# PEER expert lookup: tiles 2 to 8 gather first row halves only; second halves are read densely, times a coefficient matrix

## The reference, cut to what matters

```python
s = jnp.einsum('thpd,phkd->pthk', qh, p['pk_sub_keys'])      # scores against 2 x 128 keys
sv, si = lax.top_k(s, PK_TOPK)
cand = sv[0][..., :, None] + sv[1][..., None, :]             # 256 sums per head
best, pos = lax.top_k(cand, PK_TOPK)
eidx = ...                                                   # si[0] * 128 + si[1] of the best
gate = jax.nn.softmax(best, axis=-1)
act = jax.nn.gelu(jnp.einsum('td,thkd->thk', hb, u_tab[eb]))
out = jnp.einsum('thk,thkd->td', gb * act, v_tab[eb])
```

## Time and profile before

| | us |
|---|---|
| median of 3 runs (3966.49 to 3968.9) | 3967.75 |
| span of the profiled execution | 3962.1 |
| first dot product | 881.7 |
| DVE reads the sums of tile 1 (group 128) | 1608.3 |
| the same of tile 3 (group 256), tile 4 (group 320), tile 8 (group 576) | 2308.1, 2643.6, 3949.6 |
| PE, DVE, POOL, ACT busy | 2943.4, 2784.1, 1319.1, 676.6 |
| moved by the gathers' queue | 1208 MB |

### The profile page before, as it was taken

One profiled execution on the slowest core, in us unless ns is written; L12 is line 12 of the kernel. 1 busy time (PEld: TensorE's weight loads), 2 busy tenths in 40 slices (PEclk: granted clock), 3 DMA queues, 4 the chain that ended last, 5 costly groups with the idle time before them and its releaser, 6 DMA issues.

```text
span 3962.1 us, 46323 instructions
## 1 busy us (share of the span) xinstructions
PE 2943.4 (74%) x16906; PEld 1316.2 (33%) x16906; DVE 2784.1 (70%) x6805; ACT 676.6 (17%) x1388; POOL 1319.1 (33%) x1174
## 2 busy tenths in 40 slices
PE   8999999979899997856666666656656666665555
PEld 3666665545444442213222222212212222221111
DVE  4545647746787786756888868877877786887555
ACT  2534533011121221000111110111101111101000
POOL 0000000014444443333444444444544444444443
PEclk9999999989899998988878878878877878886777
DMA  4010004459999999999999999999999999999998
GB/s 184 23 35 26 23 25 157 170 207 410 413 415 414 408 403 415 418 423 413 414 396 413 418 416 409 416 410 420 415 411 414 418 414 408 415 416 407 418 421 343
DMA packets 214904, 1346.40 MB, mean 340 GB/s; under 512 B 24818, under 2 KB 45810, under 8 KB 63762
## 3 DMA queue, kind: packets, MB, share of 16 engines
q0 software_dynamic: 165888, 1208.03, 74.2%
q1 hardware_dynamic: 47636, 133.32, 9.0%
q10 hardware_dynamic: 1152, 2.10, 0.1%
HBM read 1329.69 MB, written 13.67 MB: 339 GB/s over the span
## 4 chain that ended last, share of the span: by engine, by line
DMA 37%; PE 35%; DVE 13%; issue 11%; POOL 2%; ACT 1%; POOLq 0%; SPq 0%; DVEq 0%; ACTq 0%
DMA arena<-in_uv,mask_b 14%; PE ps L782 12%; DMA arena<-in_uv,mask_f 12%; DMA arena<-in_uv,ones 11%; PE ps L1453 9%; DVE arena L1294 4%; PE ps L760 3%; PE ps L647 3%; POOL arena L616 2%; DVE arena L1176 2%; PE ps L1447 2%; PE ps L711 1%; PE ps L678 1%; DVE arena L1136 1%; PE ps L1505 1%
## 5 line engine op out<-in xcount | busy, mean ns | idle before, releaser
L782 PE MATMUL ps<-arena 64*64 64x512 f32 x9216 | 1461.6, 761 | 943.0 <-DVE arena L1176 929.3
L1294 DVE CUSTOM_DVE_ANT_0 arena<-arena 128x1024 f32<-128x1024 f32 x1152 | 1411.7, 1226 | 738.3 <-DMA arena<-in_uv,mask_b 285.1
L782 PEld LDWEIGHTS ps<-arena 64*64 64x64 f32 x9216 | 351.4, 158 | 1896.4 <-DVE arena L1176 1380.3
L616 POOL DMA_INDIRECT arena<-in_uv,ones x384 | 448.3, 1167 | 635.0 <-PE ps L782 467.4
L616 POOL DMA_INDIRECT arena<-in_uv,mask_f x384 | 441.8, 1150 | 586.7 <-PE ps L782 493.4
L616 POOL DMA_INDIRECT arena<-in_uv,mask_b x384 | 423.2, 1102 | 601.9 <-PE ps L782 514.6
L973 ACT ACTIVATE arena<-arena 128x2 f32<-128x2 f32 x576 | 117.3, 204 | 2641.0 <-DVE arena L1294 2565.6
L1453 PE MATMUL ps<-arena 128*128 128x384 f32 x1152 | 384.1, 489 | 1.8 <-DVE arena L1740 1.8
L1176 DVE TENSOR_SCALAR arena<-arena 128x64 f32<-128x64 f32 x1152 | 308.0, 310 | 0.3 <-ACT arena L973 0.3
L760 PE MATMUL ps<-arena 128*128 128x384 f32 x768 | 268.6, 497 | 0.0
L598 POOL IOTA arena<- 128x16 f32 x1 | 0.1, 145 | 793.3 <-PE ps L660 793.3
(11 more groups left out here) (203 smaller groups left out, 2360.7 us busy)
## 6 DMA issues: line engine op xcount, KB each, us to landing
arena<-in_w_mg SPq DMA_DIRECT2D x16, 1536.0 KB, 21.2
arena<-in_w_in SPq DMA_DIRECT2D x28, 512.0 KB, 3.3
arena<-in_w_mod SPq DMA_DIRECT2D x8, 1792.0 KB
arena<-in_w_mod SPq DMA_DIRECT2D x4, 2048.0 KB, 23.3
arena<-in_w_out SPq DMA_DIRECT2D x2, 4096.0 KB, 16.8
arena<-in_w_q SPq DMA_DIRECT2D x8, 1024.0 KB, 14.2
arena<-in_w_q SPq DMA_DIRECT2D x4, 2048.0 KB
arena<-x_scratch SPq DMA_DIRECT2D x15, 512.0 KB, 11.2
```

The costliest lines, as they stand in the source:

```text
L616: nc.gpsimd.indirect_dma_start(out=RG[n % RING], out_offset=None, in_=uv, in_offset=bass.IndirectOffsetOnAxis(ap=EIDX[t % 3][:, s:s + 1], ...
L782: mm = nc.tensor.matmul(PS[c * HALF:(c + 1) * HALF, 2 * r + n, :], DG[rows, s, :], RG[s][rows, D + n * 512:D + (n + 1) * 512], start=(g == ...
L1294: ins = v.tensor_tensor_reduce(u, u, h2, 1.0, 0.0, ALU.mult, ALU.add, PRE[:, s % RING:s % RING + 1])
```

## The change

Tiles 0 and 1 stay as they are. Tiles 2 to 8 are handled in four **teams**: (2, 3), (4, 5), (6, 7), (8).

- POOL gathers only the u halves, 4 KB a row, into six buffers `UB`. DVE's dot product frees a buffer. The dots of a tile are kept (`DOTS`); ACT takes one gelu per tile, DVE one product with the gates (`coefs`).
- When a team's dots are done, its **coefficient matrix** is built: `COEF[i2, i1, token]`, for 128 x 128 experts and up to 256 tokens. `turn` transposes key numbers and coefficients. For every four tokens (a **block**) DVE makes one-hots of both key numbers (`key_hots`, 512 columns each), ACT scales one of them (`scale_part`), PE multiplies them per token (`block`) and ACT stores the result (`block_out`). Two buffers each. There are 32 blocks a tile, two blocks a group, from `build_at(g)` = 258, 386, 514 and 638.
- Then `values`: SP loads v in 128 chunks of 128 rows (`chunk`, 0.5 MB, four buffers), PE multiplies each with the matrix. The ends of a team (`ends_at` = build_at + 112 groups) read PSUM on DVE. The matrix has one buffer, and the buffers of the ends lie in it: the next team's first block waits for the stored outputs.
- `mix`, `x1` and the norms of tiles 3 to 8 now stand at groups 117 to 156. The **late queries** of all six tiles are taken head pair by head pair (`late_query`: 384-column matmuls, weights in two buffers of 2 MB; `late_score` six per pair), every score goes through the scratch, and ACT loads it. The top-16 search of tiles 3 and 4 stands at groups 170 to 256, that of later tiles where it was. The ends of tiles 0 and 1 stand at groups 224 to 241.

```diff
+TEAMS = ((2, 3), (4, 5), (6, 7), (8,))
...
-MIX_AT, MIX_STEP = 117, 3
+MIX_AT, MIX_GAP = 117, 6
+LATE_QUERIES_AT, LATE_QUERIES_GAP = 158, 11
 EARLY_TOP_AT = {(0, 0): None, (0, 1): 0, (0, 2): 18, (0, 3): 27, (1, 0): 37, (1, 1): 47, (1, 2): 65, (1, 3): 78,
-                (2, 0): 90, (2, 1): 100, (2, 2): 110, (2, 3): 129}
-LATE_AT = {3: 2 * GROUPS + 24}
-LATE_GAP = {3: 10}
+                (2, 0): 90, (2, 1): 100, (2, 2): 110, (2, 3): 129,
+                (3, 0): 170, (3, 1): 181, (3, 2): 192, (3, 3): 203,
+                (4, 0): 214, (4, 1): 225, (4, 2): 236, (4, 3): 247}
+A_ENDS_AT = 224
...
+    VB = [hi(0), hi(1), AR[:, A_END - 2 * D:A_END - D], AR[:, A_END - D:A_END]]
+    UB = [AR[:, A_WO + n * D:A_WO + (n + 1) * D] for n in range(UR)]
+    assert A_WO + UR * D == A_END - 2 * D
+    FULL = [hi(2 + n)[:, 0:512].rearrange("p (u i) -> p u i", u=4) for n in range(2)]
+    PART = [hi(2 + n)[:, 512:1024].rearrange("p (u i) -> p u i", u=4) for n in range(2)]
...
+    def build_at(g):
+        done = (TEAMS[g][-1] + 1) * GROUPS + 2
+        return max(done, ends_at(g - 1) + 12) if g else done
...
+        return build_at(g) + 112
...
+        def query_weights(i):
+            sp.dma_start(WQB[i % 2], w_q[:, :, i * 512:(i + 1) * 512]).then_inc(l_wqb[i % 2], 16)
...
+        def chunk(g, i1):
+            n = g * P + i1
+            if n >= VR:
+                sp.wait_ge(v_done, n - VR + 1)
+            sp.dma_start(VB[n % VR], uv[i1 * P:(i1 + 1) * P, D:2 * D]).then_inc(l_v[n % VR], 16)
...
+                    if m < UR:
+                        wait_alone(pool, v_used, n + 1 - RING)
+                    else:
+                        wait_alone(pool, dots, (n - UR) // GRP + 1)
+                    nc.gpsimd.indirect_dma_start(
+                        out=UB[m % UR], out_offset=None, in_=u_rows,
+                        in_offset=bass.IndirectOffsetOnAxis(ap=EIDX[t % 3][:, s:s + 1], axis=0),
+                    ).then_inc(u_in[m % UR], 16)
...
+        def late_query(i, c, part):
+            n = (i * 4 + c) * 2 + part
+            if c == 0 and part == 0:
+                pe.wait_ge(l_wqb[i % 2], 16 + 16 * (i // 2 + 1))
+                if i == 0:
+                    pe.wait_ge(h2t_e, TILES)
+            if n >= 2:
+                pe.wait_ge(lq_e, n - 1)
+            cols = slice(part * LATE_PART, (part + 1) * LATE_PART)
             for k in range(KD):
-                mm = nc.tensor.matmul(PS[:, 4, c * P:(c + 1) * P], WQ[:, k, (i * 4 + c) * P:(i * 4 + c + 1) * P],
-                                      H2T[:, k, :], start=(k == 0), stop=(k == KD - 1))
-            if c == 3:
-                mm.then_inc(q_r, 1)
+                mm = nc.tensor.matmul(PS[:, 4 + part, 0:LATE_PART], WQB[i % 2][:, k, c * P:(c + 1) * P],
+                                      H2TB[:, k, cols], start=(k == 0), stop=(k == KD - 1))
+            mm.then_inc(lq_r, 1)
...
+        def turn(t):
+            g, j = team_of(t)
+            pe.wait_ge(coef_r, t - NA + 1)
+            if t == NA:
+                pe.wait_ge(sc_e, len(QUERY_ORDER) + PAIRS * (TILES - EARLY))
+                pe.wait_ge(lq_e, PAIRS * 8)
+            elif j == 0:
+                pe.wait_ge(tu_e, t - NA)
+            for z, x in enumerate((*KEYNO[(t - NA) % 4], DOTS[t % 2])):
+                mm = nc.tensor.transpose(PS[:, 4 + 2 * j, z * P:(z + 1) * P], x, ident[:])
+            mm.then_inc(tu_r, 1)
+        def block(g, n):
+            b_, k = n % 2, blocks_before[g] + n
+            pe.wait_ge(part_r, k + 1)
+            if k >= 2:
+                pe.wait_ge(c_r, k - 1)
+            for u in range(4):
+                mm = nc.tensor.matmul(PS[:, 5 + 2 * b_, u * P:(u + 1) * P], FULL[b_][:, u], PART[b_][:, u],
+                                      start=True, stop=True)
+            mm.then_inc(built, 1)
+        def values(g):
+            pe.wait_ge(c_r, blocks_before[g + 1])
+            if g:
+                pe.wait_ge(acc_read, TEAMS[g][0] - NA)
+            else:
+                pe.wait_ge(acc_free, 4 * NA)
+            for i1 in range(P):
+                n = g * P + i1
+                pe.wait_ge(l_v[n % VR], V_LOADS + 16 * (n // VR + 1))
+                for j in range(len(TEAMS[g])):
+                    for half in range(2):
+                        mm = nc.tensor.matmul(PS[:, 2 * j + half, :], COEF[:, i1, j * P:(j + 1) * P],
+                                              VB[n % VR][:, half * 512:(half + 1) * 512],
+                                              start=(i1 == 0), stop=(i1 == P - 1))
+                mm.then_inc(v_done, 1)
+        for g, team in enumerate(TEAMS):
+            for t in team:
+                b.at(build_at(g), lambda t=t: turn(t))
+            for n in range(len(team) * P // 4):
+                b.at(build_at(g) + 1 + n // 2, lambda g=g, n=n: block(g, n))
+            b.at(build_at(g) + 1 + len(team) * P // 8, lambda g=g: values(g))
...
+        def scale_part(g, n):
+            b_, k = n % 2, blocks_before[g] + n
+            j, q = divmod(n, P // 4)
+            act.wait_ge(oh_r, k + 1)
+            for u in range(4):
+                ins = A(PART[b_][:, u], PART[b_][:, u], ACT.Copy, scale=TURNED[j][:, 2, 4 * q + u:4 * q + u + 1])
+            ins.then_inc(part_r, 1)
+        def block_out(g, n):
+            b_, k = n % 2, blocks_before[g] + n
+            j, q = divmod(n, P // 4)
+            act.wait_ge(built, k + 1)
+            if n == 0:
+                act.wait_ge(y_st, 16 * TEAMS[g][0])
+                if g == 0:
+                    act.wait_ge(pair_done, PAIRS * EARLY)
+                    act.wait_ge(st_sc[0], 16 * (PAIRS * (TILES - 1) // 2))
+                    act.wait_ge(dots, (NA + 2) * GROUPS)
+            A(COEF[:, :, j * P + 4 * q:j * P + 4 * q + 4], PS[:, 5 + 2 * b_, :].rearrange("p (u i) -> p i u", u=4),
+              ACT.Copy).then_inc(c_r, 1)
...
+                    dve.wait_ge(v_done, (self.g + 1) * P)
+                    sums = PS[:, 2 * self.j:2 * self.j + 2, :].rearrange("p b c -> p (b c)")
+                    v.tensor_tensor(self.y, sums, G2B, ALU.mult).then_inc(acc_read, 1)
+                    dve.wait_ge(acc_read, self.t - NA + 1)
...
+        def key_hots(g, n):
+            b_, k = n % 2, blocks_before[g] + n
+            j, q = divmod(n, P // 4)
+            if n % (P // 4) == 0:
+                dve.wait_ge(tu_e, TEAMS[g][j] - NA + 1)
+            if k == 0:
+                dve.wait_ge(st_sc[1], 16 * (PAIRS * (TILES - 1) // 2))
+            elif k >= 2:
+                dve.wait_ge(built, k - 1)
+            shape = [P, 4, P]
+            want = [TURNED[j][:, z, 4 * q:4 * q + 4].unsqueeze(2).to_broadcast(shape) for z in range(2)]
+            keys_ = iota2.unsqueeze(1).to_broadcast(shape)
+            v.tensor_tensor(FULL[b_], keys_, want[1], ALU.is_equal)
+            v.tensor_tensor(PART[b_], keys_, want[0], ALU.is_equal).then_inc(oh_r, 1)
...
+            b.at((t + 1) * GROUPS, lambda t=t: coefs(t))
+        for g, team in enumerate(TEAMS):
+            for n in range(len(team) * P // 4):
+                b.at(build_at(g) + 1 + n // 2, lambda g=g, n=n: key_hots(g, n))
+            for j, t in enumerate(team):
+                end, at = End(t), ends_at(g) + 6 * j
+                for where, step in zip((at, at + 1, at + 3, at + 5),
+                                       (end.scale, end.residual, end.square, end.norm)):
+                    b.at(where, step)
...
+                    dve.wait_ge(u_in[m % UR], U_LOADS + 16 * (m // UR + 1))
+                    if s % SLOTS == 0 and t >= NA + 2:
+                        dve.wait_ge(tu_r, t - NA - 1)
+                    u, to = UB[m % UR], DOTS[t % 2][:, s % SLOTS:s % SLOTS + 1]
```

539 lines of the change are left out of this document (330 added, 209 removed).

## The result

The changed kernel takes 4568.3 us (median of 4 runs, 4565.0 to 4571.8) against 3968.3 for the kernel before (3966.5 to 3969.8): the ratio is 1.1512, with a 95% interval of 1.1496 to 1.1529. The forecast was 4510 us, or 1.137 times before, in a range of 4370 to 4760. Its direction and its range held; it was 58 us too low.

What follows compares the result with a forecast made beforehand. Before, DMA gathers were the bound, DVE with a fifth to spare. Group 258 at 2178 us, two teams of 692 (to 3562), team 2's 634 and tile 8's 307 make 4503; plus 5.6, 4510 us, range 4370 to 4760.

Steps and rivals of the forecast that it cites:

- The mechanism: Teams' stages: one matrix buffer puts build and values in series, 190 + 447 us plus 55 between teams, 692 each.
- Rival A: Team loop: values hide and the gathers bound it, 3600 us in all; chance 0.03.
- p: Values on PE: time of one f32 matmul of 128 rows and 512 columns, taken as 0.868 us.
- DVE beside the values: After a build: 80 groups take DVE 247 us, up to 320, then it waits while PE needs 447.
- Up to group 203: Stretch from group 128, over at 1613 us, through 110 us and then 250 us of late queries.
- groups 128 to 155: Tiles 4 to 8 of x1 and front: dots, one head pair, sums and ring drain, 110 us.
- groups 155 to 203: Late queries: PE sets the pace at 55 us a quarter, 250 us instead of 148 for DVE alone.
- Groups 203 to 258: All scores there: DVE's dots, five head pairs, ends of tiles 0 and 1, waits of 4; 205 us.
- Builds: Coefficient matrix, 5.4 us a group, 6.2 with a pair step: teams 0 and 1 190 us, team 2 173.
- Values: Dense chunks on PE at 3.47 us each: 447 us a team of two, 225 for tile 8, loads hidden.
- Gap: Between teams: 16 groups, two ends, rest of a pair and waits, 55 us.
- The queue rule: Dense loads beside gathers: turns between queues give up to half of 415 GB/s; the trace had SP at 150.

Runs made afterwards that it cites:

- half_values: Changed kernel without the matrix products for the second halves of the dense rows, all loads kept: 4273.4 us, ratio 1.077.
- no_build: Changed kernel without building the coefficient matrix; the values multiply a small matrix already there, in products of the same shape and number: 4006.9 us, ratio 1.010.
- half_stream: Changed kernel with only half of every dense load (256 KB a chunk instead of 512), all work and order kept: 4531.3 us, ratio 1.143.
- late_ends: Changed kernel with the ends of a team 126 instead of 112 groups after its build began, in one place, nothing left out: 4476.4 us, ratio 1.128.
- packed_build: On top of late_ends, four blocks to a group of dots instead of two, nothing left out: 4469.3 us, ratio 1.126.
- three_blocks: On top of packed_build, a third pair of one-hot tiles, with five gather ring rows instead of six: 4449.2 us, ratio 1.121.

## Why the prediction was right, and where it was off

- **The mechanism held.** Build and values stand in series on one matrix: half_values and no_build each take hundreds of microseconds off, half_stream takes only 37, and in late_ends DVE waits with its dots done. A second matrix, which would take them out of series, was in no run.
- **Rival A was right to be unlikely, and wrongly priced.** It wanted p below 0.47 us, and p was 0.87. But half_values has half the products, as if p were 0.43, and its cycle is 648 us instead of 485, its time 4273 instead of 3600. Below its point the loop does not follow the bytes; it follows the dots.
- **DVE beside the values** was the term furthest off, and it cost the forecast nothing. 80 groups were to take 247 us, up to 320; team 0's took 354 (2390 to 2744). So DVE's wait at End.scale was 111 and 110 us for teams 0 and 1 instead of 130 to 200, and 333 and 245 for team 2 and tile 8 instead of 370 and 225: 799 in all, forecast some 0.9 ms. The last gather was issued at 3892 us, forecast 3810. PE's 450 us covered all this. Where the values or the build were taken away it came to light, and half_values and no_build fell short of what was expected.
- **Up to group 203**: 1973 forecast, 1981 measured. The 8 us were lost in groups 128 to 155 (118 instead of 110); groups 155 to 203 took 251 against 250. The quarters' periods were 59.4, 57.8 and 52.7 us against 55. In each quarter PE waited for the staged scores (up to 7.6 us at a time), which was foreseen. That DVE would also wait 34 us for ScalarE's Exp, behind its copies, was not.
- **Groups 203 to 258**: 225 us instead of 205, the largest single miss. The term took two dot products at 2.3 us and 12.7 a pair, 201 in all for DVE, and 4 for waits. DVE was busy 210 us and idle 15. Both parts were too small by some 10 us: the work, for which a group had been given the pace of two undisturbed dots, and the waits, 8 us of them for gathers.
- **Builds** of teams 0 and 1: 199 and 201 instead of 190; team 2: 170 instead of 173. DVE was the bound with 195 of 199 us. That the forecast gave a group 5.4 us for the loop and not DVE's own 4.9 was right in kind: in packed_build, with fewer dots in it, two blocks take 5.7 us.
- **Values** 450 instead of 447: the 5.7 us stop was missing. Tile 8's took 242 us instead of 225: the stream ran at 278 GB/s, 1.88 us a chunk against the 1.73 of two matmuls. In half_values, where PE needs half of that, it reached 294 GB/s, 1.78 us a chunk, so four buffers alone are no faster than PE. The sum named no price for that.
- **Gap** 56 us, forecast 55.
- **The sum.** Of the 64 us or so between 4503 and the span of 4567.5, 8 were lost by group 203, 20 by group 258, 27 in two cycles of 705 and 706 instead of 692, and 9 behind group 514 (950 instead of 941). The 9 are a balance: tile 8's values cost 17 more, its build with team 2's ends 5 less, and the last end 3 less.
- **The queue rule.** half_values shows what the trace of before could not: with products that outrun it, the dense stream took 67 MB in 344 us, 195 of 404 GB/s. The Trainium skill (DMA: Bandwidth & Descriptors, "Queues, rings and completion order") has an engine take turns between queues, which would let the stream have up to half, and the trace agrees: 48%.

No version that does the whole work beats the kernel before. late_ends and three_blocks win 92 and 119 us of 600. An estimate of the least that this scheme could take: behind group 258 (2206 us) 3 x 450 + 225 of values, with the clock at its upper level and TensorE 99% busy, and some 3 x 120 + 60 of builds at ScalarE's own pace, so 4200 us. Whether one team alone in the new way, beside tiles gathered whole, would gain was not tried: the matrix takes 128 KB of each partition, the room in which the old ring lives.
